# Splitting and reordering the input projections of a hybrid S5 / HGRN2 layer on one Trainium2 core

## The chip, the cores and the metric

The kernel runs on one core of a Trainium2 chip. The metric is the device time of one execution in microseconds (us). Three runs of the kernel before took 869.65, 872.27 and 872.86 us, a median of 872.27 us. The engines are called by the names that the profile gives them: PE (TensorE; PEld is its weight load), DVE (VectorE), ACT (ScalarE), POOL (GpSimd) and SP (SyncE, which here only issues transfers).

## The reference

Two layers over 512 tokens of 1024 channels in float32. The first layer mixes the tokens with an S5 state space model and an HGRN2 mixer, the second with windowed attention, and each is followed by a mixture of 16 experts with the best two chosen. Only the first layer's mixer matters here:

```
h = rms_norm(x, even_mix_norm)
proj = h @ even_in_proj                       # 512 x 2560
u = proj[:, :512]; hq, hf, hi, hg = split(proj[:, 512:], 4)
a = s5_mixer(u)       # per step of the sequence: state = a*state + B u; y = C state + D u; gelu; gate
f = lb + (1 - lb) * sigmoid(hf); k = 1 - f; b = cumsum(log f) in chunks of 32 tokens
scores = (silu(hq) * exp(b - b_ref)) @ (k * exp(b_ref - b)).T, causal inside a chunk
state of each chunk from k * exp(b_last - b) and hi; o = scores @ hi + (silu(hq) * exp(b)) @ state
b_out = rms_norm(o) * silu(hg)
x = x + concat(a, b_out) @ even_out_proj
```

## The kernel before

**Number format.** A float32 matrix product is made either directly, or from two parts of each factor in the format fp32r: high = rounded value, low = value minus high. Three products (high x high, high x low, low x high) stand for one; each of their matmuls takes about a quarter of the time of a direct one.

**Memory.** Weights come from HBM in slots of 128 x 2048 float32 (1 MB) that SP loads into a ring of six (`ring`, L469, the first six at L436). A slot is loaded anew when `slot_free` has reached its number in the order; PE raises `slot_free` by `pending[0]` with the first matmul of a later step (`give`, L1860). Several tensors lie on the same bytes: `ring_split` on `ring`, `hT_hi` on `x`, `left_hi` on `xs`, `left_lo` on `hT`.

**Input projections.** `hT` is the normed input turned (8 blocks of 128 channels by 512 tokens). Its high part is `hT_hi` and its low part is `left_lo`. The weights of u (4 blocks of 128 outputs), of the forget gate `f` (4) and of the queries `q` (4) are blocks 0 to 11 of 128 x 1024. Block 0 is multiplied directly. For block j from 1 to 11, ACT writes the high part (`block_hi`, L782) and then minus the high part over the raw weights (`block_minus`, L787), and POOL issues a transfer that adds the raw weights from HBM to it (`block_lo`, L526), which leaves the low part. Each of these 11 transfers waits until the one before it has landed (`in_lo_in`). `split_proj(i)`, i from 0 to 7, multiplies block 4 + i (L1897); `projected(i)` on ACT (L817) takes the result out of PSUM. The values (i from 8 to 11, one for each tile of 128 tokens, L1946) use slots 6 and 7: both high parts (L868), then both minus parts (L871), then one transfer of 2 MB that adds both (L554).

**Output gate.** Projections 12 to 15 (`proj`, L1961), again one for each tile of tokens, are direct float32 products of the slots 8 and 9 with `hT_back`, which is hT_hi + left_lo, put together by one transfer of 2 MB from `hT_hi` onto `left_lo` (L558). It waits for all the values' products (`proj_psum` 12).

**S5.** PE turns the input coefficients (`turn_inputs`, L1925), multiplies (`inputs(0)`, `inputs(1)`, L1980; `make_taps`, L1991), DVE scans and forms the states, and `readout(b)` (L2004, L2012) makes the output for each quarter b. `skip(b)` on DVE adds the direct term and raises `y_sum`; ACT takes the Gelu (L886).

**HGRN2.** DVE forms `f` (`forget`) and sums its logarithm in chunks (`summed_logs`, L1353). POOL writes two differences for each head h (`differences`, L565 and L567) into `ke2` and `ke3`. ACT takes the exponentials (`exponentials`, L837 to L843) into `qe1`, `ke2`, `ke3`, DVE multiplies (`keyed`, `decayed`). `qe1`, `ke2` and later the output `o_all` lie in `x`, thus on the bytes of `hT_hi`, and for that reason POOL waits for the transfer of L558 before `differences(0)`. For each head PE makes the scores and turns the keys (`head_scores`, L2051 and L2058), the chunks' increments (`head_increments`, L2070) and the output (`head_out`, L2084 to L2090); ACT takes the turned keys out (`keys_out`, L847) and the output (`output_out`, L851). DVE chains 15 states (`states`, L1405 and L1097) and masks the scores (`causal`, L1395). The halves of projections 12 to 15 stand between these steps in PE's program. Then come the S5 gate (`glu`, L2100) and the output projection.

Every engine runs its own instructions in the order of the text, and waits at semaphores.

## Time and profile before

| what | value |
|---|---|
| median of three runs | 872.27 us |
| the profiled execution's own time | 873.5 us |
| its span (first to last instruction) | 871.7 us |
| PE busy | 778.6 us (89%) |
| DVE busy | 607.6 us (70%) |
| ACT busy | 500.6 us (57%) |
| POOL busy | 160.5 us (18%) |
| mean granted TensorE clock | 0.951 of full speed |

All times of single instructions are microseconds from the start of the span. The clock of TensorE has two levels, full (2.4 GHz) and half (1.2 GHz); a matmul at the half clock takes about twice as long. The steps that the change touches lie between 3 and 240 us.

### The profile page before, as it was taken

What the parts mean: (1) busy time and instruction counts of PE and PEld (TensorE: products, weight loads), DVE (VectorE), ACT (ScalarE), POOL (GpSimd) and SP (SyncE); (2) the same over time, 40 slices, a digit from 0 to 9 for tenths busy, and PEclk for the clock granted to TensorE, in tenths of its full rate; (3) what the DMA queues carried; (4) which work ended last, traced back from release to release, by engine and by line L of the source; (5) the groups of instructions that cost most, each with busy time, mean ns of one, the idle gap of its engine ahead of it and who ended that gap; (6) DMA issues with size and microseconds to landing.
All of it is one profiled execution on the core that took longest, in us unless ns stands there. A gap on an engine that the chain in (4) does not pass through costs nothing.

```text
span 871.7 us, 11403 instructions
## 1 busy us (share of the span) xinstructions
PE 778.6 (89%) x4356; PEld 581.3 (67%) x4356; DVE 607.6 (70%) x838; ACT 500.6 (57%) x664; POOL 160.5 (18%) x156
## 2 busy tenths in 40 slices
PE   6699969439999989998999899999999899998993
PEld 3577847325558887887877555556668878876882
DVE  5998853446565477988889645766753779887991
ACT  7358231163253247877778403787663478787881
POOL 4311000050000022322312000005100223232121
PEclk9899988759999989999999999999999899999997
DMA  9555470810147249998997700024034499989862
GB/s 369 174 95 123 99 186 8 247 42 1 50 168 292 96 180 399 367 328 313 329 322 269 291 26 0 1 97 168 26 123 186 181 394 358 334 313 324 314 212 37
DMA packets 33835, 170.91 MB, mean 196 GB/s; under 512 B 7809, under 2 KB 7937, under 8 KB 18160
## 3 DMA queue, kind: packets, MB, share of 16 engines
q1 hardware_dynamic: 18432, 130.03, 38.8%
q0 software_dynamic: 13616, 34.56, 16.3%
q10 hardware_dynamic: 1728, 5.52, 1.8%
q8 instruction: 39, 0.64, 0.3%
q14 instruction: 20, 0.16, 0.1%
HBM read 160.18 MB, written 24.12 MB: 211 GB/s over the span
## 4 chain that ended last, share of the span: by engine, by line
PE 52%; DMA 23%; DVE 8%; ACT 7%; issue 4%; POOL 2%; POOLq 2%; ACTq 1%; DVEq 0%; SPq 0%
DMA ring<-stream 16%; PE PS L2155 8%; PE PS L2404 7%; PE PS L2285 7%; PE PS L2310 5%; PE PS L1897 4%; DVE w_lo L1091 4%; PE PS L1961 4%; DMA ring_split<-stream 3%; DMA left_lo<-hT_hi 3%; ACT w_hi L743 3%; PE PS L1946 2%; PE PS L2185 2%; PE PS L2439 2%; PE PS L2100 2%
## 5 line engine op out<-in xcount | busy, mean ns | idle before, releaser
L1091 DVE TENSOR_TENSOR w_lo<-ring,w_hi 128x2048 fp32r<-128x2048 f32 x92 | 210.2, 2290 | 39.6 <-ACT w_hi L743 35.0
L743 ACT ACTIVATE w_hi<-ring 128x2048 fp32r<-128x2048 f32 x86 | 164.6, 1917 | 40.3 <-DMA ring<-stream 35.2
L2285 PE MATMUL PS<-w_hi,left_hi 128*128 128x512 f32 x512 | 174.3, 402 | 6.8 <-DVE w_lo L1091 4.8
L2285 PEld LDWEIGHTS PS<-w_hi,left_hi 128*128 128x128 f32 x512 | 96.2, 188 | 28.8 <-DVE w_lo L1091 5.1
L2285 PE MATMUL PS<-w_lo,left_hi 128*128 128x512 f32 x256 | 100.1, 391 | 0.0
L2310 PE MATMUL PS<-w_hi,left_lo 128*128 128x512 f32 x256 | 87.5, 403 | 7.2 <-DVE left_lo L1091 6.0
L2404 PE MATMUL PS<-ring,hT 128*128 128x512 f32 (+1 forms) x192 | 74.9, 535 | 0.3 <-DVE hT L1091 0.3
L591 POOL DMA_INDIRECT arena<-rows x32 | 39.5, 1233 | 129.0 <-PE PS L2262 115.6
L2310 PEld LDWEIGHTS PS<-w_hi,left_lo 128*128 128x128 f32 x256 | 49.5, 193 | 20.1 <-DVE left_lo L1091 8.1
L2404 PEld LDWEIGHTS PS<-ring,hT 128*128 128x128 f32 x192 | 35.3, 193 | 29.6 <-issue 27.7
L2285 PEld LDWEIGHTS PS<-w_lo,left_hi 128*128 128x128 f32 x256 | 48.3, 189 | 8.2
L2310 PE MATMUL PS<-w_lo,left_lo 128*128 128x512 f32 x128 | 51.2, 400 | 0.0
L2155 PE MATMUL PS<-w_lo,left_hi 128*128 128x512 f32 x128 | 50.6, 395 | 0.3 <-DVE left_lo L1091 0.3
L1897 PE MATMUL PS<-hT_hi,ring_split 128*128 128x512 f32 x144 | 39.0, 420 | 9.1 <-DMA ring_split<-stream 7.6
L2155 PE MATMUL PS<-w_hi,left_hi 128*128 128x512 f32 x112 | 44.8, 400 | 0.0
L1091 DVE TENSOR_TENSOR left_hi<-PS,left_hi 128x1024 fp32r<-128x1024 f32 (+1 forms) x35 | 40.3, 1156 | 5.4 <-ACT left_hi L938 4.6
L2155 PE MATMUL PS<-w_hi,left_lo 128*128 128x512 f32 x112 | 43.8, 391 | 0.0
L1897 PEld LDWEIGHTS PS<-hT_hi,ring_split 128*128 128x128 f32 x144 | 28.1, 201 | 17.6 <-DMA ring_split<-stream 9.7
L817 ACT ACTIVATE arena<-PS 128x512 f32<-128x512 f32 x16 | 9.5, 607 | 52.0 <-PE PS L1897 20.5
L1097 DVE SCALAR_TENSOR_TENSOR arena<-const,PS 128x256 f32<-128x256 f32 x64 | 26.4, 475 | 17.5 <-PE PS L2439 17.5
L595 POOL DMA_INDIRECT out<-hT,rows x16 | 25.8, 1615 | 66.6 <-ACT hT L954 66.6
L681 POOL TENSOR_TENSOR arena<-arena,small 128x1024 f32<-128x1024 f32 x8 | 15.2, 1896 | 121.7 <-DVE small L1779 121.7
(301 smaller groups left out, 1479.3 us busy)
## 6 DMA issues: line engine op xcount, KB each, us to landing
ring<-stream SPq DMA_DIRECT2D x110, 1024.0 KB, 16.4
arena<-stream SPq DMA_DIRECT2D x6, 1024.0 KB, 8.8
ring_split<-stream POOLq DMA_DIRECT2D x11, 512.0 KB, 5.5
rows<-arena POOLq DMA_DIRECT2D x8, 512.0 KB, 3.0
x<-stream SPq DMA_DIRECT2D x4, 1024.0 KB, 6.7
x<-x_in SPq DMA_DIRECT2D x4, 512.0 KB, 5.3
ring_split<-stream POOLq DMA_DIRECT2D x1, 2048.0 KB, 13.4
left_lo<-hT_hi POOLq DMA_DIRECT2D x1, 2048.0 KB, 24.6
```

Of the source, the lines that this page charges most:

```text
L591: return pool.indirect_dma_start(xrow[j], None, rows_d[:, :], bass.IndirectOffsetOnAxis(index, 0), bounds_check=SEQ - 1, oob_is_err=False)
L595: return pool.indirect_dma_start((sums_d, out_d)[layer][:, :], bass.IndirectOffsetOnAxis(index, 0), rows, None, bounds_check=SEQ - 1, oob_ ...
L743: act.activation(w_hi[pair], held_slot(layer, m), ACT.Copy).then_inc(w_hi_done, 1)
L1091: return V.tensor_tensor(out, a, b, op)
L1097: return V.scalar_tensor_tensor(out, a, s, b, op0, op1)
L1897: ins = mm(out, w[:, k, :], h[:, k, :], start=t == 0 and k == 0, stop=t == 2 and k == KD - 1)
L1946: ins = mm(out, h[:, k, m], w, start=t == 0 and k == 0, stop=t == 2 and k == KD - 1)
L1961: ins = mm(PS[:, 7, :], hT_back[:, k, m], k512(s + k // 4)[:, k % 4, :], start=k == 0, stop=k == KD - 1)
L2155: ins = mm(mixed(layer, s // 2, tt), a, b, start=k == 0 and n == 0, stop=k == KD - 1 and n == 2)
L2285: ins = mm(PS[:, gate_bank(e), :], a, b, start=k == 0 and t == 0, stop=k == KD - 1 and t == 2)
L2310: ins = mm(PS[:, y_at(layer, e) + half, :], a, b, start=k == 0 and t == 0, stop=k == 1 and t == 2)
L2404: ins = mm(PS[:, 2 + part, 0:n], hT[:, k, tt * 128:tt * 128 + 128], w, start=k == 0, stop=k == KD - 1)
```

## The change

It has seven parts.

1. **Two low parts in flight.** `in_lo_in` becomes two semaphores used in turn, and transfer n of the low parts waits for n - 2 instead of n - 1. The high and minus parts' counts are renumbered (`high_made`), since the semaphore `hT_split` is folded into `in_split` and `coefs_done`.
2. **Slots 4 and 5 later.** SP loads them once the second block of u is in PSUM (`u_psum` 2), no longer at the start.
3. **Two gate blocks moved up.** `split_proj(2)` goes ahead of `turn_inputs`, into PSUM bank 3, and `split_proj(3)` ahead of `inputs(0)`; the steps behind them move by one, so that between `inputs(1)` and `readout(0)` only `split_proj(7)` is left. ACT's high and minus parts of blocks 9 and 10 go one step earlier too.
4. **Values by halves.** Slots 6 and 7 are split one by one: high, minus and a 1 MB transfer for slot 6 after `projected(5)`, and for slot 7 after `projected(7)`. PE takes all three products of the first half, then two of the second, and its last one at the end. `readout(2)` stands between values 10 and 11.
5. **The input's two parts are summed per two row tiles.** Two transfers of 1 MB instead of one of 2 MB: tokens 0 to 255 after values 8 and 9, tokens 256 to 511 after values 10 and 11. A row of one transfer is now 256 elements. Projections 12 and 13 need the first, 14 and 15 the second.
6. **Queries and keys in freed weight slots.** `qe1` and `ke2` move to ring slots 0 and 1 (`o_all` stays in `x`), so `differences(0)` waits for the values' products and not for a sum. ACT waits for both sums before the first `output_out`. The slots 12 and 13 of the weights are loaded with the first matmul of `proj(15)` and no longer from `readout(2)` on; slots 10 and 11 are given free at `readout(3)`.
7. **Order of the heads.** PE: `proj(12)` and `proj(13)` whole ahead of `head_scores(0)`, then halves of 14 and 15 between the heads. ACT: all values are taken out before the logarithm, then the four Gelus (after `y_sum` 4), then all exponentials, then `keys_out(0)`. DVE: `skip(3)` goes ahead of `summed_logs(0)`.

```diff
+        def proj_bank(i):
+            return 3 if i == 2 else 7 if i >= 14 else 6 + i % 2
+        def high_made(j):
+            return 2 * j if j > 1 else 1
+        def low_in(engine, n):
+            engine.wait_ge(in_lo_in[n % 2], 16 * (n // 2 + 1))
...
-        qe1, ke2, ke3 = cut(x_t, 0, HEADS, 512), cut(x_t, 2048, HEADS, 512), cut(xs_t, 0, HEADS, 512)
+        qe1, ke2, ke3 = cut(ring, 0, HEADS, 512), cut(ring, SLOT, HEADS, 512), cut(xs_t, 0, HEADS, 512)
-        o_all = qe1
+        o_all = cut(x_t, 0, HEADS, 512)
...
             for j in (2, 3, 0, 1, 4, 5):
+                if j == 4:
+                    sp.wait_ge(u_psum, 2)
                 sp.dma_start(slot(j), stream_d[j, :, :]).then_inc(slot_full[j], 16)
...
-                pool.wait_ge(in_split, 2 * j)
-                if j >= 2:
-                    pool.wait_ge(in_lo_in, 16 * (j - 1))
+                pool.wait_ge(in_split, 2 * j + 1)
+                if j >= 3:
+                    low_in(pool, j - 3)
...
-            pool.wait_ge(in_split, 26)
-            pool.wait_ge(in_lo_in, 16 * 11)
-            pool.dma_start(ring_split[:, 0:2 * SLOT].rearrange("p (s n) -> p s n", n=SLOT), stream_d[6:8, :, :].rearrange("s p n -> p s n"),
-                           accum_op=ALU.add).then_inc(in_lo_in, 16)
-            pool.wait_ge(proj_psum, 12)
-            pool.wait_ge(in_lo_in, 16 * V_LO)
-            pool.dma_start(left_flat_lo.bitcast(f32), hi_flat.bitcast(f32), accum_op=ALU.add, max_dma_last_dim=4096).then_inc(in_lo_in, 16)
+            for half in range(2):
+                n = V_LO + half
+                pool.wait_ge(in_split, V_HIGH + 2 * half + 1)
+                low_in(pool, n - 2)
+                pool.dma_start(v_lo(half), stream_d[6 + half, :, :], accum_op=ALU.add).then_inc(in_lo_in[n % 2], 16)
+            for half in range(2):
+                n, m = HT_BACK + half, slice(256 * half, 256 * half + 256)
+                pool.wait_ge(proj_psum, 10 + 2 * half)
+                low_in(pool, n - 2)
+                pool.dma_start(hT_back[:, :, m], hT_hi.bitcast(f32)[:, :, m], accum_op=ALU.add).then_inc(in_lo_in[n % 2], 16)
...
             pool.wait_ge(state_done, 4)
-            pool.wait_ge(in_lo_in, 16 * HT_BACK)
+            pool.wait_ge(proj_psum, 12)
             differences(0)
...
-            for j in range(5, 9):
+            for j in range(5, 10):
                 block_hi(j)
                 block_minus(j)
...
+            for i in range(3, 12):
                 projected(i)
+                if i == 3:
+                    block_hi(11)
+                    block_minus(11)
+                if i in (5, 7):
+                    values_hi((i - 5) // 2)
...
+            act.wait_ge(y_sum, 4)
             for b in range(4):
-                act.wait_ge(y_sum, b + 1)
                 act.activation(catT[:, b, :].rearrange("p (c s) -> p s c", s=STEP),
...
+            for h in range(HEADS):
+                exponentials(h)
+            keys_out(0)
+            projected(12)
+            projected(13)
+            keys_out(1)
+            output_out(0)
...
             split_proj(0)
             split_proj(1)
+            split_proj(2)
             turn_inputs()
-            split_proj(2)
+            split_proj(3)
+            pending[0] = 2
             pe.wait_ge(u_done, 4)
+            pe.wait_ge(proj_done, 3)
             pe.wait_ge(bT_done, 2 * STEP)
             inputs(0)
-            split_proj(3)
-            pending[0] = 2
             split_proj(4)
+            split_proj(5)
             make_taps()
-            split_proj(5)
+            split_proj(6)
             inputs(1)
-            split_proj(6)
             split_proj(7)
             pending[0] = 2
             readout(0)
+            first, second = [(0, 0), (0, 1), (0, 2), (1, 0), (1, 1)], [(1, 2)]
+            split_values(8, first)
+            split_values(9, first)
+            split_values(8, second)
+            split_values(9, second)
             readout(1)
-            split_values(10, (0, 1, 2))
-            split_values(11, (0, 1, 2))
-            pending[0] = 4
+            split_values(10, first + second)
             readout(2)
+            split_values(11, first + second)
+            pending[0] = 2
             readout(3)
...
+            proj(12)
+            proj(13)
             head_scores(0)
-            proj(12, low)
             head_increments(0)
-            proj(12, high)
             head_scores(1)
-            proj(13, low)
+            proj(14, low)
             head_out(0)
             head_increments(1)
-            proj(13, high)
             head_scores(2)
-            proj(14, low)
+            proj(14, high)
             head_out(1)
             head_increments(2)
-            proj(14, high)
             head_scores(3)
             proj(15, low)
             head_out(2)
```

## Rows read from the trace of the kernel before

**Rows 1.** The page, busy us (share of the span) xinstructions of each engine.

```profile
PE 778.6 (89%) x4356; PEld 581.3 (67%) x4356; DVE 607.6 (70%) x838; ACT 500.6 (57%) x664; POOL 160.5 (18%) x156
```

**Rows 2.** Waits of PE, 22 to 240 us: us in total, times, longest.

```profile
PE PS L2051 <- DVE x L1091: 21.9, 1, 21.9
PE PS L1946 <- DMA ring_split<-stream: 10.2, 1, 10.2
PE PS L1897 <- DMA ring_split<-stream: 7.6, 5, 4.1
PE PS L1961 <- ACT arena L817: 3.3, 1, 3.3
```

**Rows 3.** Timeline of PE, blocks of u and gate: start, us, what, [idle before, releaser].

```profile
32.44 3.60 PE L1897 MATMUL PS<-hT_hi,ring_split 128*128 128x512 f32 x8 [1.87 <-DMA ring_split<-stream]
...
41.97 3.33 PE L1897 MATMUL PS<-hT_hi,ring_split 128*128 128x512 f32 x8 [4.11 <-DMA ring_split<-stream]
...
54.60 3.93 PE L1897 MATMUL PS<-hT_hi,ring_split 128*128 128x512 f32 x16 [1.16 <-DMA ring_split<-stream]
```

**Rows 4.** Timeline of POOL, 20 to 37 us.

```profile
22.03 1.10 POOL L526 DMA_DIRECT2D ring_split<-stream  x1 [0.94 <-ACT in_hi L782]
32.65 3.92 POOL L548 TENSOR_TENSOR xs<-const,small 128x2048 f32<-128x2048 f32 x1 [9.52 <-DMA arena<-cread]
36.52 0.91 POOL L526 DMA_DIRECT2D ring_split<-stream  x1
```

**Rows 5.** The page, DMA issues: count, KB each, median us from issue to landing.

```profile
ring_split<-stream POOLq DMA_DIRECT2D x11, 512.0 KB, 5.5
...
ring_split<-stream POOLq DMA_DIRECT2D x1, 2048.0 KB, 13.4
left_lo<-hT_hi POOLq DMA_DIRECT2D x1, 2048.0 KB, 24.6
```

**Rows 6.** Busy by stretch: PE, PEld, DVE, ACT, POOL; clock, DMA share, GB/s.

```profile
0.00:30.00 30.00, 20.54 (x79) 13.57 (x80) 19.31 (x55) 23.08 (x32) 11.90 (x44) 1.00 0.95 366
```

**Rows 7.** Timeline of ACT, the values' high and minus parts.

```profile
111.32 3.70 ACT L868 ACTIVATE ring_split<-ring 128x2048 fp32r<-128x2048 f32 x2
115.11 3.72 ACT L871 ACTIVATE ring_split<-ring_split 128x2048 fp32r<-128x2048 f32 x2
```

**Rows 8.** The chain that ended last, 119 to 200 us: start, us, what.

```profile
132.53 6.50 PE PS L1946 x16
...
143.05 11.16 PE PS L1946 x48
```

**Rows 9.** Timeline of ACT, exponentials and Gelus.

```profile
181.34 0.63 ACT L837 ACTIVATE x<-x 128x512 f32<-128x512 f32 x1 [15.92 <-POOL xs L567]
...
184.41 0.62 ACT L837 ACTIVATE x<-x 128x512 f32<-128x512 f32 x1
...
193.59 1.28 ACT L886 ACT_TABLE_LOAD   x1
194.89 3.92 ACT L886 ACTIVATE arena<-arena 128x512 f32<-128x512 f32 x4
```

**Rows 10.** Timeline of PE, the heads.

```profile
190.66 6.38 PE L1961 MATMUL PS<-ring,left_lo 128*128 128x512 f32 x8 [3.34 <-ACT arena L817]
...
201.61 1.05 PE L2051 MATMUL PS<-x 128*128 128x128 f32 x8
...
202.93 3.60 PE L1961 MATMUL PS<-ring,left_lo 128*128 128x512 f32 x8
206.46 0.44 PE L2088 MATMUL PS<-arena 128*32 128x128 f32 x8
...
209.37 1.17 PE L2070 MATMUL PS<-arena 32*128 32x128 f32 x30
```

**Rows 11.** Timeline of DVE, the states of head 0 and what follows.

```profile
198.20 0.29 DVE L1405 COPY arena<-PS 128x128 f32<-128x128 f32 x1 [6.00 <-PE PS L2070]
...
204.31 0.89 DVE L1395 COPY_PREDICATED arena<-const,PS 128x128 f32<-128x128 int32 x4
```

More of the change, by code:

```diff
@@ L790, in _ @@
             act.wait_ge(hT_done, 2 * TT)
-            act.activation(hT_hi[:, 0:4, :], hT[:, 0:4, :], ACT.Copy).then_inc(hT_split, 1)
+            act.activation(hT_hi[:, 0:4, :], hT[:, 0:4, :], ACT.Copy).then_inc(in_split, 1)
             act.wait_ge(turns_done, TURN)
@@ L857, in gate_out, with values_hi @@
                 act.activation(uT[:, b, :], PS[:, (0, 1, 4, 5)[b], :], ACT.Sigmoid).then_inc(glu_sig, 1)
-            for i in range(2, 10):
-                projected(i)
-                if i in (2, 3):
-                    block_hi(8 + i)
-                    block_minus(8 + i)
-                if i == 7:
-                    for s in range(2):
-                        loaded_v, nth = filled(6 + s)
-                        act.wait_ge(loaded_v, 16 * nth)
-                        act.activation(v_hi(s), slot(6 + s), ACT.Copy).then_inc(in_split, 1)
-                    act.drain()
-                    for s in range(2):
-                        act.activation(v_lo(s), v_hi(s), ACT.Copy, scale=-1.0).then_inc(in_split, 1)
+            def values_hi(half):
+                loaded_v, nth = filled(6 + half)
+                act.wait_ge(loaded_v, 16 * nth)
+                act.activation(v_hi(half), slot(6 + half), ACT.Copy).then_inc(in_split, 1)
+                act.drain()
+                act.activation(v_lo(half), v_hi(half), ACT.Copy, scale=-1.0).then_inc(in_split, 1)
+            for i in range(3, 12):
+                projected(i)
+                if i == 3:
[3 more added lines that the diff above has]
+                    values_hi((i - 5) // 2)
                 if i == 4:
@@ L888, in _ @@
                     .then_inc(gelu_done, 1)
-            for h in range(HEADS - 1):
-                projected(12 + h)
-                keys_out(h + 1)
-                output_out(h)
+            for h in range(HEADS):
[5 more added lines that the diff above has]
+            output_out(0)
+            keys_out(2)
+            projected(14)
+            output_out(1)
+            keys_out(3)
+            output_out(2)
             projected(15)
@@ L1202, in _ @@
                 ks = slice(4 * half, 4 * half + 4)
-                dve.wait_ge(hT_split, 2)
-                tt_(left_lo[:, ks, :], hT[:, ks, :], hT_hi[:, ks, :], ALU.subtract).then_inc(hT_split, 1)
+                dve.wait_ge(in_split, HT_HIGH)
+                tt_(left_lo[:, ks, :], hT[:, ks, :], hT_hi[:, ks, :], ALU.subtract).then_inc(coefs_done, 1)
             br = par("b_re").rearrange("p (a b) -> p a b", b=32)
@@ L1368, in _ @@
             forget()
+            skip(3)
             summed_logs(0)
             summed_logs(1)
-            skip(3)
             summed_logs(2)
@@ L1928, in split_proj @@
             def split_proj(i):
-                if i >= 2:
+                if i >= 3:
                     pe.wait_ge(proj_done, i - 1)
-                block_products(4 + i, PS[:, 6 + i % 2, :]).then_inc(proj_psum, 1)
+                if i == 2:
+                    pe.wait_ge(u_done, 2)
+                block_products(4 + i, PS[:, proj_bank(i), :]).then_inc(proj_psum, 1)
             def split_values(i, terms):
                 m, out = slice(128 * (i - 8), 128 * (i - 8) + 128), PS[:, 6 + i % 2, :]
-                if 0 in terms:
+                if (0, 0) in terms:
                     pe.wait_ge(proj_done, i - 1)
-                for t in terms:
-                    for k in range(KD):
-                        if t == 0 and k % 4 == 0:
-                            pe.wait_ge(in_split, 23 + k // 4)
-                        if t == 2 and k == 0:
-                            pe.wait_ge(in_lo_in, 16 * V_LO)
-                        h, w = (hT_hi, left_lo, hT_hi)[t], (v_hi, v_hi, v_lo)[t](k // 4)[:, 512 * (k % 4):512 * (k % 4) + 512]
+                for half, t in terms:
+                    if t == 0:
+                        pe.wait_ge(in_split, V_HIGH + 2 * half)
+                    if t == 2:
+                        low_in(pe, V_LO + half)
+                    for k in range(4 * half, 4 * half + 4):
+                        h, w = (hT_hi, left_lo, hT_hi)[t], (v_hi, v_hi, v_lo)[t](half)[:, 512 * (k % 4):512 * (k % 4) + 512]
                         ins = mm(out, h[:, k, m], w, start=t == 0 and k == 0, stop=t == 2 and k == KD - 1)
-                if 2 in terms:
+                if (1, 2) in terms:
                     ins.then_inc(proj_psum, 1)
```

50 lines of the change are left out of this document (23 added, 27 removed).

## The prediction

> **What bounds the kernel now.** I read the page first: PE is busy for 778.6 of 871.7 us [rows 1]. So nearly all that can be won is idle time of PE and matmuls at the half clock behind it. All seven parts lie before 240 us, so I asked next for the waits of PE between 22 and 240 us. Four kinds make up 43.0 us [rows 2]: 21.9 for the first scores, 10.2 for the values' low part, 7.6 in five waits for the low parts of blocks, and 3.3 for ACT to take a projection out. Then the chain and the timelines tell what stands behind each.
>
> The 21.9 us are the sum hT_hi + left_lo: 24.6 us from issue to landing [rows 5], nothing of PE beside it but the last readouts, because `ke2` lies on its source and POOL waits for it; only then come differences, exponentials, `keyed` and the scores. The 10.2 us are a 2 MB transfer of 13.4 us [rows 5] that was issued only when ACT had written two high and two minus parts (111.32 to 118.83) [rows 7]. The waits for blocks come from a start in single file: the transfer of the second block stands on POOL behind L548, which begins at 32.65 since the read coefficients land then, and each later one waits for its forerunner [rows 4].
>
> **Half clock.** Eight of these matmuls take 11.16 / 48 x 8 = 1.86 us [rows 8]. After idle time they take longer: 3.60 and 3.33 us for eight [rows 3], 6.50 instead of 3.72 for sixteen [rows 8], and half a `proj` takes 6.38 instead of 206.46 - 202.93 = 3.53 [rows 10]. That is 1.7, 1.5, 2.8 and 2.8 us on top of the waits.
>
> **The change part by part.** PE does the same matmuls, so the sum counts waits removed and waits made.
>
> *Start (parts 1 to 3).* Up to 30 us the transfers run at 366 GB/s [rows 6]. With slots 4 and 5 (2.1 MB) held back, what ACT has queued should land 2.1 / 0.366 = 5.7 us earlier; I take 5, so L548 runs from 27.6 to 31.5. The first block's low part, issued at 22.03 [rows 4] and used at 32.44, was slowed by the same loads, so its wait of 1.87 and its slow matmuls (1.7) go [rows 3]. The second block's transfer leaves at 31.4 and takes 5.5 [rows 5], landing at 36.9. PE is there at 30.6 + 2 x 1.86 = 34.3 and waits 2.6 instead of 4.1 [rows 3]. The third leaves 0.9 us later. The price of a further block on a running queue is not in the trace; the two sizes give (13.4 - 5.5) / 1.5 MB = 5.3 us per MB and 2.8 us fixed [rows 5], so it lies between 2.6 (fixed part overlapped) and 5.5 (nothing overlapped). I take 2.6: landing 39.5, PE ready at 40.6. The wait of 1.16 for the fourth block goes too. Together 1.9 + 1.7 + 1.5 + 1.2 = 6.3. Slots 4 and 5 now start at about 33, just beside these two transfers; I take off 1.0. Bounds: 2.5 (the loads hold up both) to 9 (no wait at all). Moving `split_proj(2)` and `(3)` up adds one wait: `split_proj(3)` needs the second result out of PSUM instead of the first after `turn_inputs`, one more copy on ACT, 0.5 us. I cost the rest of the reorder at nothing. `inputs(0)` moves behind one block more, and so ends about when it does now; DVE's way from there to the first states lies under `split_proj(4)` to `(7)`, 4 x 24 x 0.2325 = 22 us with `make_taps` and `inputs(1)` on top. Without that cover the next thing late would be `state_done` 1, and `readout(0)` by what is missing. Start: 6.3 - 1.0 - 0.5 = **4.8 us**.
>
> *Values (part 4).* Slot 6's chain runs under blocks 10 and 11. Let R be the start of `readout(0)`. ACT takes projection 7 out (0.6), writes high and minus of slot 7 (1.9 + 1.9) [rows 7], and the 1 MB transfer takes 2.8 + 5.3 = 8.1: it lands at R + 12.5. PE has the readout, 143.05 - 139.03 = 4.0, and five of the six parts of values 8 and 9, of four matmuls each: 40 x 0.2325 = 9.3 [rows 8], so it asks at R + 13.3. Slots 8 and 9 are loaded just then and may add up to 2; I take a wait of 0.5. Removed: 10.2 + 2.8. Values: **12.5 us**, bounds 10 and 13.
>
> *Sums and places (parts 5 and 6).* Let T be the end of `readout(3)`. The first half leaves after values 9, some 24 us before T, and is needed at T. The second leaves 4 us before T and is needed by `proj(14)`, which comes at T + 21 (below): 25 us. What a half costs is bounded by the 1 MB that the fit gives, 8.1, and the 24.6 that the whole took while four slots were loaded beside it [rows 5]. The half has rows of 1 KB, so if it went by pieces it could cost more (a rival below); I take 12.3, half of 24.6, and both ends keep it hidden, as 24.6 just fits. POOL now starts `differences(0)` after the values, behind the issue of the second half (1 to 2.5 us of POOL), while the logarithm and its sums on DVE are later anyway.
>
> The Trainium skill, *DMA: Bandwidth & Descriptors*, Rules for kernel authors, says of two transfers to disjoint halves that they use the same engines, serialize and are not worth the trouble. It also gives (Anatomy of one DMA) about 2.0 us plus bytes at 436 GB/s, which makes 3.2 us for a block where this trace has 5.5, so the trace does not bear out its rate for adding transfers. By it a half would take 4.4 us; the sum stays as it is.
>
> *Heads (part 7).* Of the waits, 21.9, 3.3 and the slow 2.8 go: 28.0. The new order, from T: `skip(3)` 0.75, Gelus 3.92, a table load 1.28, then exponentials. One head's take 184.41 - 181.34 = 3.07 [rows 9], all four 12.3, then `keys_out(0)` 0.6: done at T + 18.8. The Gelus stood behind the exponentials before; their 5.2 us are now ahead of them, and `keyed` and `head_scores` wait behind. PE meanwhile has `proj(12)` and `(13)`, 4 x 3.53 = 14.1 and little more, and `head_scores(0)`, 202.93 - 201.61 = 1.3 [rows 10]: it arrives at T + 15.9 and waits **2.9**. `head_increments` then ends at T + 19.9. From there DVE needs 204.31 - 198.20 = 6.1 for the states [rows 11]; PE fills this with scores (1.3) and one half of a projection (3.5), where it had two halves before. So it waits 1.3 ahead of each of three `head_out`: **3.9**. (DVE's other work for a head, some 4.3 us, fits into `head_out` 2.9 plus increments 1.1 [rows 10] but for 0.3, in two of them: 0.6.) After the wait of 2.9 some matmuls may run at the half clock: 1.0. Heads: 28.0 - 2.9 - 3.9 - 0.6 - 1.0 = **19.6 us**, bounds 14 and 24.
>
> *Behind the heads.* Slots 12 to 14 are loaded together when `proj(15)` begins; ACT wants slot 12 some 14 us later (two half projections, the output, the increments, ACT's slot 11), and three slots at 366 GB/s [rows 6] with the fixed 2.8 take 11.4. I cost it at nothing; if it took 20, ACT's next instructions, the glu's gates, would be 6 late. All later loads are released by steps that shift with the rest, so the gain is kept.
>
> **Sum.** 4.8 + 12.5 + 19.6 = 36.9, and 1.0 more that goes at the start: the two smaller waits, 7.6 less the three of [rows 3], 0.5, and a third of the 1.5 of slow matmuls, 0.5: 37.9. The profiled execution took 873.5, 1.8 more than its span: 873.5 - 37.9 = 835.6. It is 1.2 above the median, so I predict **835 us**.
>
> **Rivals.**
> - *The low parts do not overlap, or slots 4 and 5 hold them up* (chance 0.14). For it: they share all engines at 366 GB/s. Against it: the fixed 2.8 us should overlap. The start then gives 2 instead of 5.8: 839. By the skill's rule above, taken for the low parts too, this is what would happen.
> - *The heads fall to the half clock* (0.12). For it: four waits in 45 us, and the clock fell after waits of 1.87 and 4.11 [rows 3]. Against it: the three later waits are 1.3. If half of the 33 us between the first increments and the gate ran slow, with DVE's states unchanged, PE's share of about 27 us would grow by some 13: 849.
> - *Slot 12 or the gates come late* (0.08): 841.
> - *Less waiting than I take* (0.10): the exponentials of the first head suffice early enough and the start loses every wait: 829.
> - *The halves cost by piece* (0.03, the other side). A half has 1 KB rows where the whole had pieces four times that. At p us per half with both in one queue, the first is late by p - 24, the second by p - 21. It eats the 37.9 from p = 41.5 on. At four times the price per byte, p = 49: 53 us lost, 889. Against it: the 512 KB blocks and the 2 MB lie on one line of bytes [rows 5].
> - *No change* (0.01): only if PE's waits were an artefact; the chain runs through them.
>
> **Numbers.** The forecast has 0.52. The range 827 to 848 takes in the first, third and fourth rivals and half of the second. No measurement here tells less than about 0.5% (4.4 us) from no change; all cases but the piece rival and an unforeseen stall lie beyond it: faster 0.95, same 0.02, slower 0.03.
>
> **What would show it.** L1946 has no wait over 1 us; the wait of 21.9 at L2051 is gone; the sum's transfers land under readouts and projections; PE waits about 3 us before the first increments and 1 to 2 before each output; exponentials follow Gelus; u's low parts land in pairs some 3 us apart; `glu` begins at about 201 instead of 239. The prediction is wrong if a half takes over 25 us, if PEclk shows half in the heads, or if a new wait stands between `glu` and the experts.

## The result and the profile after

The changed kernel takes **836.5 us** (median of four runs, 834.6 to 839.4) against 871.5 us for the kernel before on the same chip (four runs): a ratio of 0.960, 95% interval 0.957 to 0.964. It is faster by 4.0%, 1.5 us above the 835 that was predicted. The profiled execution has a span of 835.3 us where it had 871.7, and a mean granted clock of 0.977 where it had 0.951.

The page, busy time of each engine, of the kernel after:

```profile
PE 773.3 (93%) x4356; PEld 579.2 (69%) x4356; DVE 608.6 (73%) x838; ACT 499.8 (60%) x664; POOL 166.1 (20%) x158
```

The matmuls are as many as in [rows 1] and PE is busy 5.3 us less, so 31 of the 36.4 us that the span lost were idle time of PE, and the rest is matmuls that no longer run at the half clock. The waits of PE from 22 to 215 us, total, times and longest, show which:

```profile
PE PS L1921 <- DVE left_lo L1115: 3.8, 2, 2.8
PE PS L2101 <- ACT arena L865: 3.7, 1, 3.7
PE PS L1921 <- ACT arena L834: 2.0, 1, 2.0
PE PS L2119 <- DVE arena L1121: 1.5, 1, 1.5
PE PS L2119 <- DVE xs L1121: 1.5, 1, 1.5
PE PS L1972 <- DMA ring_split<-stream: 1.0, 1, 1.0
```

Of the four kinds of [rows 2], 43.0 us, the one for scores (21.9) is gone, that for the values' low part has fallen from 10.2 to 1.0, those for the blocks' transfers (7.6) are gone, and so is the 3.3 for ACT. In their place stand 3.7 us ahead of the first increments (L2101), twice 1.5 us ahead of outputs (L2119), and one that was not predicted, 3.8 us for `left_lo` (0.8 before). The wait for ACT ahead of `split_proj(3)` is 2.0 us; before, that of the same kind was

```profile
PE PS L1897 <- ACT arena L817: 1.6, 1, 1.6
```

The timeline of PE places them; `readout(0)` begins with the row at 105.77, `readout(3)` ends with the one at 143.91, and `glu` begins at 201.38:

```profile
31.18 1.20 PE L1921 MATMUL PS<-left_lo,in_hi 128*128 128x512 f32 x4 [2.76 <-DVE left_lo L1115]
33.38 2.07 PE L1921 MATMUL PS<-left_lo,in_hi 128*128 128x512 f32 x4 [1.00 <-DVE left_lo L1115]
35.25 3.61 PE L1921 MATMUL PS<-hT_hi,ring_split 128*128 128x512 f32 x8
...
68.32 2.11 PE L1921 MATMUL PS<-hT_hi,ring_split 128*128 128x512 f32 x8 [2.04 <-ACT arena L834]
...
105.77 2.32 PE L2031 MATMUL PS<-arena 128*128 128x512 f32 x8
...
120.25 2.11 PE L1972 MATMUL PS<-ring_split,hT_hi 128*128 128x512 f32 x8 [0.96 <-DMA ring_split<-stream]
...
143.91 1.94 PE L2039 MATMUL PS<-arena 128*32 128x127 f32 x64
145.78 14.00 PE L1988 MATMUL PS<-ring,left_lo 128*128 128x512 f32 x32
...
164.81 1.47 PE L2101 MATMUL PS<-arena 32*128 32x128 f32 x30 [3.70 <-ACT arena L865]
166.21 2.08 PE L2080 MATMUL PS<-ring 128*128 128x128 f32 x8
...
201.38 13.90 PE L2131 MATMUL PS<-arena,ring 128*128 128x512 f32 x32
```

Laid against the same steps of the kernel before, this gives the gain stage by stage:

| stage | before, us | after, us | gain | predicted |
|---|---|---|---|---|
| start of the span to `readout(0)` | 110.6 | 105.8 | 4.9 | 5.8 |
| `readout(0)` to the end of `readout(3)` | 51.8 | 40.1 | 11.7 | 12.5 |
| end of `readout(3)` to `glu` | 76.4 | 55.5 | 20.8 | 19.6 |
| `glu` to the end | 632.9 | 633.9 | -1.0 | 0 |

The page's DMA issues show the halves' transfers (count, KB each, median us to landing):

```profile
ring_split<-stream POOLq DMA_DIRECT2D x11, 512.0 KB, 5.6
...
ring_split<-stream POOLq DMA_DIRECT2D x2, 1024.0 KB, 8.9
left_lo<-hT_hi POOLq DMA_DIRECT2D x2, 1024.0 KB, 12.1
```

The half of the sum was costed at 12.3 and takes 12.1 (10.2 and 14.0 us); the half of the values was costed at 8.1 and takes 8.9 by the median (8.2 and 9.6; PE waits for the one of 9.6). PE waits for neither half of the sum.

### The profile page after: what moved, and what is told of

It is laid out like the page before. It is cut to its first block, busy times and chain, and to the rows that moved or that the text cites. A ratio compares the mean times of both kernels' runs of the same rounds, so it can differ in the third digit from the quotient of the medians.

```text
span 835.3 us, 11410 instructions
## 1 busy us (share of the span) xinstructions
PE 773.3 (93%) x4356; PEld 579.2 (69%) x4356; DVE 608.6 (73%) x838; ACT 499.8 (60%) x664; POOL 166.1 (20%) x158
## 3 DMA queue, kind: packets, MB, share of 16 engines
q0 software_dynamic: 15184, 34.56, 17.2%
## 4 chain that ended last, share of the span: by engine, by line
PE 42%; DMA 20%; DVE 19%; issue 7%; ACT 7%; POOL 2%; DVEq 1%; ACTq 0%; POOLq 0%
DMA ring<-stream 17%; DVE w_lo L1115 9%; PE PS L2184 8%; PE PS L2433 7%; PE PS L2314 4%; ACT w_hi L760 3%; PE PS L2339 3%; DMA ring_split<-stream 3%; PE PS L2468 2%; PE PS L2131 2%; PE PS L1972 2%; PE PS L1921 2%; DVE arena L1121 2%; PE PS L2214 1%; PE PS L2491 1%
## 5 line engine op out<-in xcount | busy, mean ns | idle before, releaser
L2433 PEld LDWEIGHTS PS<-ring,hT 128*128 128x128 f32 x192 | 35.2, 193 | 29.3 <-issue 27.6
L1921 PE MATMUL PS<-hT_hi,ring_split 128*128 128x512 f32 x144 | 37.3, 407 | 2.0 <-ACT arena L834 2.0
L834 ACT ACTIVATE arena<-PS 128x512 f32<-128x512 f32 x16 | 9.3, 613 | 49.9 <-PE PS L1972 29.7
L962 ACT ACTIVATE left_hi<-PS 128x1024 fp32r<-128x1024 f32 x30 | 30.3, 1009 | 8.4 <-PE PS L2291 8.4
## 6 DMA issues: line engine op xcount, KB each, us to landing
left_lo<-hT_hi POOLq DMA_DIRECT2D x2, 1024.0 KB, 12.1
```

The source lines that it names most:

```text
L962: act.activation(row_hi[j], PS[:, 0:2, :].rearrange("p a (b c) -> p (a b) c", c=128), ACT.Copy)\
L1921: ins = mm(out, w[:, k, :], h[:, k, :], start=t == 0 and k == 0, stop=t == 2 and k == KD - 1)
L2433: ins = mm(PS[:, 2 + part, 0:n], hT[:, k, tt * 128:tt * 128 + 128], w, start=k == 0, stop=k == KD - 1)
```

## Experiments: what each part is worth

Each kernel below ran beside the kernel before; the ratio of the two carries the interval, and the lower it is the faster the kernel. The changed kernel itself was timed a second time, beside three of these, at 836.9 us; differences in us are those of the medians against it.

### The changed kernel once more

> The changed kernel unaltered, for a comparison on the same chip with the versions below. Both theories: 836 to 837, ratio 0.960.

Measured: 836.9 us, ratio 0.962 (0.959 to 0.964). Two measurements of one kernel lie 0.3 us apart (836.88 and 836.54), and the interval is 2 us wide to either side. An effect smaller than that can't be told from nothing here.

### The sum as one transfer

```diff
-            for half in range(2):
-                n, m = HT_BACK + half, slice(256 * half, 256 * half + 256)
-                pool.wait_ge(proj_psum, 10 + 2 * half)
-                low_in(pool, n - 2)
-                pool.dma_start(hT_back[:, :, m], hT_hi.bitcast(f32)[:, :, m], accum_op=ALU.add).then_inc(in_lo_in[n % 2], 16)
+            pool.wait_ge(proj_psum, 12)
+            low_in(pool, HT_BACK - 2)
+            low_in(pool, HT_BACK - 1)
+            pool.dma_start(left_flat_lo.bitcast(f32), hi_flat.bitcast(f32), accum_op=ALU.add, max_dma_last_dim=4096)\
+                .then_inc(in_lo_in[HT_BACK % 2], 16)
...
```

> The changed kernel with the two half sums made one transfer of 2 MB again, after the last values; queries and keys stay in the ring slots, so the differences don't wait for it. It leaves at 142.1 and takes between 13.4 (the values' 2 MB before) and 24.6 (this sum before, with four slots loaded beside it; here two), say 18. Theory: proj(12) waits for it from 145.8 to about 160, and since the exponentials are ready by then, the wait of 3.7 before the first increments goes: about 11 us lost, 847. If only the wait for ke2 mattered, as part 6 alone would have it, proj(12) hardly waits and the time is 836 to 839.

Measured: 854.1 us, ratio 0.981 (0.978 to 0.983), 17.2 us slower than the changed kernel. The timeline of PE:

```profile
162.22 15.94 PE L1987 MATMUL PS<-ring,left_lo 128*128 128x512 f32 x32 [15.61 <-DMA left_lo<-hT_hi]
```

The wait is the whole landing, 19.1 us from the issue at 142.9, less the last readout, and the projections behind it begin at the half clock (0.50 granted from 162 to 166 us): 15.94 us for what took 14.00. That is 7 us worse than the 847 expected, in which the transfer was taken at 18 us and no half clock was reckoned. The 3.7 us ahead of the increments were to be given back; 3.0 of them were, and one more wait of 1.5 ahead of an output (three instead of two) took half of that again. The step of the prediction that the halves matter because one of them lands before the last readout is shown.

### Queries and keys back in x

```diff
-        qe1, ke2 = cut(ring, 0, HEADS, 512), cut(ring, SLOT, HEADS, 512)
+        qe1, ke2 = cut(x_t, 0, HEADS, 512), cut(x_t, 2048, HEADS, 512)
...
-            pool.wait_ge(proj_psum, 12)
+            low_in(pool, HT_BACK)
+            low_in(pool, HT_BACK + 1)
             differences(0)
```

> The changed kernel with part 6 undone: qe1 and ke2 lie in x again, and POOL waits for both half sums before the first difference. In the changed kernel the first difference starts at 147.98, and the second half sum leaves at 142.12 and takes 14.0. Theory: the places are worth what the wait costs, so the differences start at about 156.5, the wait of PE before the first increments grows from 3.7 to about 12, glu begins at about 209.5 instead of 201.4, and the time is about 844.5 (changed kernel 836.5). Rival: PE's two whole projections before the heads cover the sum anyway; then the time stays at 836 to 838.

Measured: 842.7 us, ratio 0.968 (0.964 to 0.971). POOL's first difference, and PE's waits behind it:

```profile
157.34 1.07 POOL L582 TENSOR_TENSOR x<-arena 128x512 f32<-128x512 f32 x1 [12.80 <-DMA left_lo<-hT_hi]
```

```profile
PE PS L2102 <- ACT arena L866: 7.5, 1, 7.5
...
PE PS L2081 <- DVE x L1116: 1.8, 1, 1.8
```

`differences(0)` begins at 157.3 instead of 148.0, and the wait ahead of the increments grows from 3.7 to 7.5, not to the 12 that was expected. `glu` comes 7.4 us later, 0.9 of which already stand ahead of the heads (their first projection begins at 146.6 instead of 145.8). So the places are worth about 6 us, and not all 9.4 of the delay: the eight differences take 11.0 us here and 13.6 in the changed kernel. All of that lies in the first three, which DVE's scans run beside there, while DVE is idle here; the other five take the same in both.

### Values split whole

One transfer of 2 MB for both slots after `projected(7)`, as before, and PE takes all low products last.

```diff
-                if i in (5, 7):
-                    values_hi((i - 5) // 2)
+                if i == 7:
+                    values_hi()
...
-            first, second = [(0, 0), (0, 1), (0, 2), (1, 0), (1, 1)], [(1, 2)]
+            first, second = [(0, 0), (1, 0), (0, 1), (1, 1)], [(0, 2), (1, 2)]
```

> The changed kernel with part 4's halves undone: both high parts, both minus parts and one 2 MB transfer after projection 7, and PE takes the low products of values 8 and 9 last. With R the start of readout(0), the transfer leaves at R + 8.7 and lands at R + 22; PE asks at R + 11.7, so it waits about 10 us and then runs some matmuls at the half clock (2.8 more), where the changed kernel waits 1.0. Theory: +11.5, 848. Rival: the time that PE loses here is given back at the heads, where PE waits for exponentials (3.7) whatever it does before; then +8 or less, 844.

Measured: 848.8 us, ratio 0.974 (0.971 to 0.978), 12 us slower than the changed kernel. The wait is that of [rows 2] again, 9.8 us where it was 10.2:

```profile
PE PS L1973 <- DMA ring_split<-stream: 9.8, 1, 9.8
```

It stands behind the high and the `left_lo` products of values 8 and 9, the sixteen matmuls after it take 6.03 us (3.72 by [rows 8]), and nothing later gives it back: the wait ahead of the increments is 3.7 us as before. The term of 12.5 us is shown.

### Gelus behind the exponentials

```diff
+            for h in range(HEADS):
+                exponentials(h)
+            keys_out(0)
             act.wait_ge(y_sum, 4)
...
-            for h in range(HEADS):
-                exponentials(h)
-            keys_out(0)
```

> The changed kernel with ACT's four Gelus and their table load behind the exponentials and the first keys_out, as before the change. The prediction put the Gelus' 5.2 us in front of keys_out(0): by that the wait of 3.7 before the first increments goes and the time is about 833. Rival, from the trace of the changed kernel: ACT waits 0.20, 0.85 and 0.25 for POOL's differences between the heads' exponentials, so POOL paces them (its last difference ends at 161.6) and the Gelus lie in a hole; then the wait stays between 3 and 4 and the time is 836 to 837, or more by up to 4 if projection 12 now comes out of PSUM after the Gelus.

Measured: 842.9 us, ratio 0.968 (0.966 to 0.971). This is where a step of the prediction fell. It said that the Gelus' 5.2 us, now ahead of the exponentials, are what `head_increments(0)` waits for. With them behind, the wait is the same:

```profile
PE PS L2101 <- ACT arena L865: 3.7, 1, 3.7
PE PS L1988 <- ACT arena L834: 3.4, 1, 3.4
```

The timeline of ACT in this kernel shows both sides:

```profile
152.68 0.63 ACT L855 ACTIVATE ring<-ring 128x512 f32<-128x512 f32 x1 [4.75 <-POOL xs L584]
...
165.72 1.28 ACT L905 ACT_TABLE_LOAD   x1
167.02 3.90 ACT L905 ACTIVATE arena<-arena 128x512 f32<-128x512 f32 x4
...
172.23 1.08 ACT L834 ACTIVATE arena<-PS 128x512 f32<-128x512 f32 x2
```

Without Gelus ahead of them the exponentials idle 4.75 us for POOL's differences and begin no earlier than in the changed kernel (152.3). What paces them is POOL. In the changed kernel, timeline of ACT:

```profile
152.26 0.63 ACT L855 ACTIVATE ring<-ring 128x512 f32<-128x512 f32 x1
...
155.13 0.63 ACT L855 ACTIVATE ring<-ring 128x512 f32<-128x512 f32 x1 [0.20 <-POOL xs L584]
...
158.67 0.63 ACT L855 ACTIVATE ring<-ring 128x512 f32<-128x512 f32 x1 [0.85 <-POOL xs L584]
...
161.59 0.63 ACT L855 ACTIVATE ring<-ring 128x512 f32<-128x512 f32 x1 [0.25 <-POOL xs L584]
```

and timeline of POOL:

```profile
147.98 1.81 POOL L582 TENSOR_TENSOR ring<-arena 128x512 f32<-128x512 f32 x1 [4.30 <-DVE arena L1377]
149.76 1.95 POOL L584 TENSOR_TENSOR xs<-arena 128x512 f32<-128x512 f32 x1
...
160.07 1.49 POOL L584 TENSOR_TENSOR xs<-arena 128x512 f32<-128x512 f32 x1
```

The exponentials of the second to fourth head start within 0.05 us of the end of the head's last difference, and ACT was idle for 0.2 to 0.9 us until then. Only the first head's start 0.5 us after it (it ends at 151.7), when ACT has loaded its table. The Gelus fill time that ACT had to wait anyway. Behind the exponentials they cost some 6 us, more than the 4 that was thought the most, since `projected(12)` and `(13)` then stand behind them: PE waits 3.4 us for the bank, and the eight matmuls after that take 6.74 us instead of 3.60.

### Slots 4 and 5 at the start

```diff
             for j in (2, 3, 0, 1, 4, 5):
-                if j == 4:
-                    sp.wait_ge(u_psum, 2)
```

> The changed kernel with slots 4 and 5 loaded at the start again. Theory: the read coefficients land at about 32 and no longer at 24, the second block's low part leaves at 36.5, u ends at about 49.4 instead of 46.2, readout(0) starts at about 109 instead of 105.8, and the time is 839.5. DVE's left_lo is then ready at 29.3 and not at 33.3, since POOL's large product no longer runs beside it. Rival: the two effects cancel, 836 to 837.

Measured: 841.2 us, ratio 0.965 (0.962 to 0.968), 4.3 us slower than the changed kernel by the medians. By the ratios it is 3.2, and the two intervals overlap, but each of its four runs (840.5 to 843.9) lies above all nine of the changed kernel (834.6 to 839.4). POOL's second issue of blocks stands at 36.23, near the 36.52 of [rows 4], instead of 27.90, and PE waits for the low part of the second block, timeline of PE:

```profile
41.56 3.78 PE L1919 MATMUL PS<-hT_hi,ring_split 128*128 128x512 f32 x8 [5.37 <-DMA ring_split<-stream]
```

`readout(0)` begins at 109.3 instead of 105.8. So 3.5 of the start's gain of 4.9 us come from this part.

### Low parts in single file, and the gates' blocks back

```diff
                 pool.wait_ge(in_split, 2 * j + 1)
-                if j >= 3:
-                    low_in(pool, j - 3)
+                if j >= 2:
+                    low_in(pool, j - 2)
```

> The changed kernel with the low parts of the blocks in single file again (transfer n waits for n - 1); everything else stays. By the prediction's sum the third block's low part would land up to 2.9 us later and cost up to 2: 838. Rival, from the changed trace: PE asks for it only at 44.4, long after it landed, because what PE waits for at the start is left_lo from DVE; then readout(0) starts at 105.8 as before and the time is 836 to 837.

Measured: 838.9 us, ratio 0.962 (0.959 to 0.965). PE has hardly a wait for a block's low part here either: its weight loads wait 1.0 us in two (0.2 in one in the changed kernel), which leaves two gaps of 0.2 and 0.3 us between matmuls. The transfers leave so early, once the loads are out of the way, that they have landed nearly in time one by one. Still `readout(0)` begins at 107.6, 1.8 us later than in the changed kernel. What differs is the clock behind an equal wait, timeline of PE:

```profile
68.50 3.13 PE L1921 MATMUL PS<-hT_hi,ring_split 128*128 128x512 f32 x8 [2.04 <-ACT arena L834]
```

After the same 2.04 us of idle time the eight matmuls took 2.11 us in the changed kernel and 3.13 in this one, and the next eight 2.61 instead of 1.98. The half clock behind this wait stands in five of the twelve profiled runs that have it, among them the one with the sum as one transfer (3.59 us), whose edit lies far behind; so it can come without a cause in the edit. Whether the two small gaps have a part in it here is not shown. The overlap is worth 2 us at most, which can't be told from nothing.

The second kernel undoes the third part of the change: `split_proj(2)` and `(3)` behind `turn_inputs` and `inputs(0)`, and ACT's splitting of blocks 9 to 11 as before.

> The changed kernel with part 3 undone: split_proj(2) behind turn_inputs in bank 6, split_proj(3) behind inputs(0), and ACT's blocks 9 and 10 one step later. Theory: the move costs one more copy of 0.5 us after turn_inputs and gives nothing that PE waits for, so readout(0) starts at 105.3 to 105.8 and the time is 836. Rival: with inputs(0) 5.6 us earlier the first products or sines are late and PE waits for them at inputs(1): 838 to 840.

Measured: 835.5 us, ratio 0.958 (0.955 to 0.961); the wait for ACT (L834) is 1.5 instead of 2.0 us. The part was costed at a loss of 0.5 and is worth nothing that can be measured.

## Experiments: the wait that was not predicted

At the start PE waits 3.8 us for `left_lo`, which DVE forms, and then works at the half clock (0.50 granted from 33 to 38.6 us): 2.07 us for four matmuls and 3.61 for eight, in the timeline above; eight take 1.86 by [rows 8]. DVE itself is held up. Its timeline in the changed kernel:

```profile
24.12 3.86 DVE L1115 TENSOR_TENSOR small<-small,param 128x16 f32<-128x16 f32 x4
...
28.83 4.49 DVE L1115 TENSOR_TENSOR left_lo<-hT,hT_hi 128x2048 fp32r<-128x2048 f32 x2 [0.17 <-issue]
```

Four operations on 128x16 took 3.86 us, and their shortest, median and longest durations (ns), by source, are:

```profile
L1115 DVE TENSOR_TENSOR small<-small,param x4: 167/172/3596, 24.1 to 24.4; 128x16 f32<-128x16 f32 x4
```

One of them lasted 3596 ns in place of 170. Beside it ran POOL's large product, L562, started just ahead of it, by tile:

```profile
L562 POOL TENSOR_TENSOR xs<-const,small x1: 3614/3614/3614, 24.3 to 24.3; 128x2048 f32<-128x2048 f32 x1
```

The product is L548 of [rows 4]. With slots 4 and 5 out of the way the read coefficients land sooner and it begins at 24.3, not 32.7, now ahead of `left_lo` in DVE's program. The same product held DVE up in the kernel before as well, at another place in its program. Twelve small operations there took 5.13 us and take 1.71 in the changed kernel (DVE's timelines, before and after):

```profile
33.01 5.13 DVE L1091 TENSOR_TENSOR small<-small 128x16 f32<-128x16 f32 x12
...
37.02 1.71 DVE L1115 TENSOR_TENSOR small<-small 128x16 f32<-128x16 f32 x12
```

That was behind `left_lo`, and PE was not waiting for it. Theory: the small operation is held for the whole of POOL's instruction. Rival: DVE was waiting for something else, and the order of the two does not matter.

### The product behind the low part

```diff
-            block_lo(1)
+            for j in range(1, 4):
+                block_lo(j)
+            pool.wait_ge(coefs_done, HT_LO + 1)
...
-            for j in range(2, 12):
+            for j in range(4, 12):
                 block_lo(j)
```

> A new version: POOL issues the low parts of blocks 1 to 3 first and starts its large product (turn_hi times the steps, 3.6 us) only when left_lo is done. In the changed kernel it runs from 24.34 to 27.95, and in this stretch four small operations of DVE take 3.86 us where the kernel before took 0.43. Theory: POOL's product holds DVE up, so left_lo is ready at 29.3 instead of 33.3; PE's waits of 2.76 and 1.00 shrink to 0.8, u ends at about 40 to 41 instead of 46.2, and readout(0) starts 5 to 6 us earlier: 831. Rival: the small operations were slow because of the transfers landing at that time, or DVE's chain to the first states (busy until 77 in every version) becomes the bound: 835 to 837.

Measured: 831.7 us, ratio 0.954 (0.951 to 0.957), 5 us faster than the changed kernel, and `readout(0)` at 101.3 instead of 105.8. DVE's timeline, POOL's, and PE's wait:

```profile
25.53 4.49 DVE L1117 TENSOR_TENSOR left_lo<-hT,hT_hi 128x2048 fp32r<-128x2048 f32 x2 [0.17 <-issue]
```

```profile
30.11 3.99 POOL L564 TENSOR_TENSOR xs<-const,small 128x2048 f32<-128x2048 f32 x1 [0.22 <-DVE left_lo L1117]
```

```profile
PE PS L1923 <- DVE left_lo L1117: 0.8, 1, 0.8
```

The low part ends 3.3 us earlier and PE's wait for it falls from 3.8 to 0.8 us. The edit also issues the second and third blocks' transfers ahead of the product, since they would else leave only behind it. That alone is not the gain: PE waited for none of them in the changed kernel. The hold-up is not gone but moved to where nothing waits for it, view by source:

```profile
L1117 DVE TENSOR_TENSOR arena<-param,small x4: 682/683/4108, 29.9 to 35.2; 128x512 f32<-128x512 f32 x4
```

Now an operation on 128x512, which takes 683 ns by its median, takes 4108 beside the product. The theory stands: wherever the product is put, the DVE operation beside it is lengthened by the same amount, 3.42 us before (5.13 less 1.71), 3.43 in the changed kernel (3596 less 170 ns) and 3.43 here (4108 less 683 ns). The rival is refuted, too: the order of the two is what moved `left_lo`. Nor was it a transfer beside them: here POOL issues one at 23.96, and the four small operations from 24.25 take 0.43 us. The Trainium skill, *SBUF — State Buffer*, "SBUF: two separate sides", says that a DVE operation with two SBUF inputs and a POOL operation that reads SBUF share a port pair as an exclusive lock: whichever starts first has it for the whole instruction, and the other is blocked. This case's traces agree: the small operation, started just behind the product of 3614 ns, ended with it, after 3596 ns.

### The product in quarters

```diff
+            for q in range(4):
+                i4 = slice(4 * q, 4 * q + 4)
+                ins = nc.gpsimd.tensor_tensor(cosT.rearrange("p (i c) -> p i c", c=NSTEP)[:, i4, :], at_step[:, i4, :],
+                                              turn_hi[:, i4].unsqueeze(2).to_broadcast([P, 4, NSTEP]), ALU.mult)
```

> The changed kernel with POOL's large product cut into four of a quarter each, at the same place. Theory (POOL's instruction holds DVE's out until it ends): a small operation of DVE is held up by at most one quarter, 0.9 us, at a time, its longest falls from 3.6 to about 1, and left_lo is ready up to 2.5 us earlier, if DVE gets in between the quarters: 834 to 836. Rival (DVE is held out for as long as POOL has such work queued, or by the transfers): the stretch of DVE stays at 3.6 us in all and the time at 836.5.

Measured: 836.3 us, ratio 0.960 (0.958 to 0.962), no different from the changed kernel. By source:

```profile
L564 POOL TENSOR_TENSOR xs<-const,small x4: 1038/1064/1067, 24.7 to 27.7; 128x512 f32<-128x512 f32 x4
```

```profile
L1118 DVE TENSOR_TENSOR small<-small,param x4: 165/173/1036, 24.5 to 25.7; 128x16 f32<-128x16 f32 x4
L1118 DVE TENSOR_TENSOR small<-small x7: 163/170/869, 23.9 to 27.7; 128x16 f32<-128x16 f32 x7
...
28.05 5.09 DVE L1118 TENSOR_TENSOR left_lo<-hT,hT_hi 128x2048 fp32r<-128x2048 f32 x2 [0.17 <-issue]
```

The longest hold-up of a small operation falls to one quarter's duration, but the quarters hold up one DVE operation after the other, the last of them `left_lo` itself (5.09 us instead of 4.49, last row, from the timeline). Beside the four, DVE loses 2.9 us in all instead of 3.4, and the low part ends at 33.1 against 33.3, though this profile stands 0.4 us later at 24 us. The hold-up goes by instruction; shorter pieces share it out and remove little of it.

## Experiments: the wait ahead of the first increments

`keys_out(0)` stood behind the exponentials of all four heads, and these end with POOL's last difference. If the fourth head's go behind `keys_out(1)`, the wait of 3.7 us should go.

```diff
-            for h in range(HEADS):
+            for h in range(HEADS - 1):
                 exponentials(h)
             keys_out(0)
             projected(12)
             projected(13)
             keys_out(1)
+            exponentials(HEADS - 1)
             output_out(0)
```

> A new version of ACT's order at the heads: keys_out(0), projections 12 and 13 and keys_out(1) go ahead of the exponentials of head 3, which DVE needs only some 18 us later; it costs one more pair of table loads (2 x 1.28). In the changed kernel ACT reaches keys_out(0) at 164.2, PE asks from 161.1. Theory: ACT reaches it at 161.1, PE's wait of 3.7 shrinks to below 1, and glu begins 3 us earlier: 833.5. Rival: PE then waits the same time at proj(14) or head_out(0) for the table loads or for the states, or the exponentials of head 3 come too late for its scores: 836 to 838.

Measured: 835.6 us (six runs, 831.1 to 839.6), ratio 0.959 (0.956 to 0.962). The wait went as expected, but the time can't be told from the changed kernel's:

```profile
PE PS L2120 <- DVE arena L1122: 2.6, 2, 1.6
...
PE PS L2102 <- ACT arena L865: 0.8, 1, 0.8
```

In its place came a third wait ahead of an output (2.6 in two for `arena`, where it was 1.5 in one) and one of 0.6 ahead of the scores. From the end of `readout(3)` to `glu` it takes 54.1 us instead of 55.5. Alone this experiment decides nothing; with the product moved as well:

> The versions of e8 (POOL's large product after left_lo) and e10 (keys first) together. Theory: the two gains lie in different stages and add up, 4.8 + 3: 828.5. Rival: DVE, busy without a pause until 77 and nearly so from there to the first states, takes back part of the first: 831.

Measured: 829.5 us, ratio 0.954 (0.951 to 0.956); its profiled span is 826.0 us at a clock of 0.984, and `glu` begins at 192.8. Timeline of PE:

```profile
156.25 1.17 PE L2104 MATMUL PS<-arena 32*128 32x128 f32 x30 [0.77 <-ACT arena L867]
```

This is the fastest kernel of the study, 7 us under the changed one, with an interval apart from that of its second timing. Against the product moved alone (831.7) it is 2.3 us by the medians and nothing by the ratios (0.954 both), so the runs don't tell the two apart. The profiles do in the stage that was changed: from the end of `readout(3)` to `glu` this kernel takes 52.6 us and the other 56.2.

## Why the prediction was right

Point by point, by its own steps:

- **What bounds the kernel.** Right. The waits that were named are the ones that went, and what each of the first three stages gained is PE's idle time and the half clock behind it. The step from the sum to the forecast has a slip: 835.6 less 1.2 is 834.4, not 835. The kernel's 836.5 is 2.1 us from that.
- **Values, 12.5.** Right, 11.7. PE waits 1.0 us and not 0.5; the transfer that it waits for takes 9.6 and not 8.1 (up to 2 more was allowed for). Splitting them whole gives the 12 us back.
- **Sums by halves.** Right: 12.1 by the median against 12.3, and both hidden. The rival in which halves cost by the piece is refuted: 41.5 us or more were needed, 14.0 is the longest. Two transfers of a half each are no faster than one (12.1 + 12.1 against 19.1 us from issue to landing when the whole was sent in the experiment above), but the first leaves earlier, and that is worth 17.2 us, the half clock behind the long wait included. The Trainium skill, *DMA: Bandwidth & Descriptors*, Rules for kernel authors, says of two transfers to disjoint partition halves that they serialize and are not worth it; these halves are of tokens, on all partitions, and the rule says nothing about when each may start.
- **Heads, 19.6.** The size is right, 20.8. The wait ahead of the increments was put at 2.9 and is 3.7, but its cause was wrong: "their 5.2 us are now ahead of them, and `keyed` and `head_scores` wait behind" is the step that failed. POOL's differences pace the exponentials, and without the Gelus ahead of them the wait is still 3.7. That the size came out is luck. The prediction had `keys_out(0)` done at T + 18.8 (T is the end of `readout(3)`, 145.85 here), by ACT's work alone, and it was done at T + 18.9 (164.8), by POOL's. The 3.07 us for one head's exponentials, from [rows 9], hold a copy of 0.6 out of PSUM that no longer stands there; four heads take ACT 10.6 and not 12.3, and waiting for POOL (0.20, 0.85 and 0.25) makes up 1.3 of the difference. PE asks at T + 15.3 instead of T + 15.9, hence 3.7. The waits ahead of outputs were put at 4.5 in three and are 3.1 in two. The slow matmuls are 1.0 us for L2080 (2.08 against 1.05 in [rows 10]), 0.3 for L2101 and 0.4 for L2089 (1.02 against 0.60), where 1.0 was taken. And the 28.0 that go leave out 1.5 us: the first scores and turned keys ran slow in the kernel before (2.08 and 1.06 us). With these the terms give 28.0 + 1.5 - 3.7 - 3.1 - 1.7 = 21.0.
- **Start, 5.8.** The size is near, 4.9, by another way. The prediction had the product (L548 before) start at 27.6; it started at 24.3, so the blocks' transfers left 3.5 us earlier than it took and no wait of 2.6 for the second block is left. But it did not look at what a product begun that early would hold up: 3.8 us of waits for `left_lo` and the half clock behind them. The two errors nearly cancel, and that is luck: with the product behind the low part `readout(0)` begins at 101.3, a gain of 9.3 us. The price of a further block on a running queue was taken at 2.6 us and measures 2.7: the second and third land at 33.2 and 35.9. But that this price decides the start, and the rival by which the low parts do not overlap, both missed the place: in single file the low parts are late by 0.5 us at most.
- **The gates' blocks, -0.5, and what stands behind the heads, 0.** Right within what can be measured: 0.5 us more of a wait for ACT (2.04 against 1.56), and from `glu` on 1.0 us longer than before.

What stays open: why one wait of 2.04 us for ACT is followed by the half clock in some runs (2.83 to 3.62 us for eight matmuls) and not in others (2.11); no run was made for that.

## What to carry to other kernels

When a transfer or an ordering keeps a long wait, look first for the part of it that can leave earlier (a half, another place in memory), and cost the change by who asks when, not by the transfer's own speed. When loads are moved and a step of another engine thereby starts sooner, ask what that step holds up at its new time: here a product of POOL that held DVE up at 32.7 us, when PE needed nothing of it, cost some 5 us at 24.3. And when an engine has idle time ahead of a wait, check who releases it before blaming the work that stands there: taking the Gelus away left the wait as it was, since POOL was the pace.

## What the hardware showed that was not expected

A DVE operation of two SBUF inputs on 128x16, 170 ns by itself, takes 3596 ns when a POOL product of 3614 ns started just ahead of it; one on 128x512 takes 4108 instead of 683 ns beside the same product of 3.99 us; with the product in four instructions of 1.06 us the longest is 1036 ns. With DVE's scans both sides are slower, and by less: POOL's first three differences on 128x512 take 1.81, 1.95 and 1.99 us beside them and 1.07, 1.03 and 1.06 with DVE idle, and the four scans take 6.20 us instead of the 4.56 with POOL idle.
